# The lags of the filter: stored in the order of the products, or in the order of time

## The reference

```python
def hyena_filter_spectra(L, w_in, w_hid, b, freq, w_out):
    ...
    for k, w in enumerate((w_in, w_hid[0], w_hid[1])):
        hdn = jnp.sin(freq[k] * (hdn @ w.astype(f32) + b[k]))
    h = (hdn @ w_out.astype(f32)).reshape(L, HY_ORDER, 2, HY_WIDTH)
    ...
    h = h * jnp.exp(-t * deltas)[:, None, None, :]
    hf, hb = h[:, :, 0], h[:, :, 1]
    k_circ = jnp.concatenate([hf[:1] + hb[:1], hf[1:], jnp.zeros_like(hf[:1]), hb[:0:-1]], axis=0)
    return jnp.fft.rfft(k_circ, axis=0)
```

## Time and profile before

| | us |
|---|---|
| median of three runs | 4332.37 |
| the profiled execution | 4332.37 |
| its span | 4330.7 |
| outside the span | 1.67 |
| TensorE busy | 3802.4 (88%) |
| VectorE busy | 1439.4 (33%) |
| ScalarE busy | 899.4 (21%) |

### The profile page before, as it was taken

The page is one execution under the profiler, slowest core; times in us unless marked ns, Lnnn a source line. Parts: engine busy times, 40 slices in busy tenths (PEclk is TensorE's granted clock), DMA queues, the critical chain, the costliest instruction groups (busy, mean ns, idle before and its releaser), DMA issues. The chain is left out here.

```text
span 4330.7 us, 47795 instructions
## 1 busy us (share of the span) xinstructions
PE 3802.4 (88%) x18109; PEld 2658.2 (61%) x18109; DVE 1439.4 (33%) x2293; ACT 899.4 (21%) x1423; POOL 304.7 (7%) x278
## 2 busy tenths in 40 slices
PE   8798999994899999999978586998799959999995
PEld 2587888882666776677656354676466734444442
DVE  3124445445333443344333442232311241111112
ACT  1323333322122222122212242101111120000000
POOL 0400000000000000000000000221210000000001
PEclk9899999996999999999999687999899969999997
DMA  9100000101100000000011400001211128888885
GB/s 337 54 10 26 16 1 16 64 20 47 56 27 27 0 27 26 26 1 26 26 70 51 186 0 25 20 19 58 59 44 54 39 94 333 332 340 338 334 338 219
DMA packets 160410, 410.13 MB, mean 95 GB/s; under 512 B 14345, under 2 KB 97399, under 8 KB 147703
## 3 DMA queue, kind: packets, MB, share of 16 engines
q1 hardware_dynamic: 147244, 361.93, 22.9%
q0 software_dynamic: 8064, 29.36, 1.9%
q10 hardware_dynamic: 4972, 16.90, 1.0%
HBM read 347.35 MB, written 58.72 MB: 94 GB/s over the span
## 5 line engine op out<-in xcount | busy, mean ns | idle before, releaser
L1615 PE MATMUL hyena_up<-aT,ring 128*128 128x512 f32 x1024 | 465.6, 610 | 67.5 <-DMA ring<-in_hy_w_in 67.5
L1615 PEld LDWEIGHTS hyena_up<-aT,ring 128*128 128x128 f32 x1024 | 196.4, 197 | 298.0 <-issue 298.0
L1592 DVE COPY ring<-hyena_bank 128x512 f32<-128x512 f32 x192 | 131.9, 691 | 294.4 <-PE hyena_bank L1657 116.3
L2196 PE MATMUL hgrn_proj<-xT,ring 128*128 128x512 f32 x384 | 169.4, 600 | 9.8 <-DMA ring<-in_w_in 9.8
L3026 DVE TENSOR_TENSOR moe_h<-moe_gate,moe_up 128x512 f32<-128x512 f32 x32 | 22.0, 689 | 420.0 <-PE moe_up L2937 420.0
L1116 PE MATMUL mla_scores<-ring,mla_v 128*128 128x128 f32 x1280 | 153.8, 275 | 3.7 <-DVE ring L1019 3.7
L1116 PEld LDWEIGHTS mla_scores<-ring,mla_v 128*128 128x128 f32 x1280 | 148.0, 192 | 4.7 <-DVE ring L1019 4.7
L1519 ACT ACTIVATE ring<-hyena_bank 128x512 f32<-128x512 f32 x192 | 115.9, 603 | 164.1 <-PE hyena_bank L1657 60.4
L2196 PEld LDWEIGHTS hgrn_proj<-xT,ring 128*128 128x128 f32 x384 | 73.0, 193 | 97.7 <-issue 97.7
L1636 PE MATMUL hyena_bank<-ring,hyena_fwd 128*128 128x128 f32 x1088 | 126.6, 276 | 0.3
L1636 PEld LDWEIGHTS hyena_bank<-ring,hyena_fwd 128*128 128x128 f32 x1088 | 124.0, 192 | 2.3 <-DVE hyena_conv L1565 1.9
(11 more groups left out here) (548 smaller groups left out, 7452.5 us busy)
## 6 DMA issues: line engine op xcount, KB each, us to landing
ring<-in_w_gate_experts SPq DMA_DIRECT2D x16, 2048.0 KB
ring<-in_w_up_experts SPq DMA_DIRECT2D x16, 2048.0 KB, 17.1
ring<-in_w_down_experts SPq DMA_DIRECT2D x16, 2048.0 KB
aT<-in_w_gate_experts SPq DMA_DIRECT2D x16, 2048.0 KB, 12.9
aT<-in_w_up_experts SPq DMA_DIRECT2D x16, 2048.0 KB, 17.4
moe_w_spare<-in_w_down_experts SPq DMA_DIRECT2D x16, 2048.0 KB, 9.0
ring<-in_ada_w SPq DMA_DIRECT2D x12, 2048.0 KB, 9.4
ring<-in_hy_w_in SPq DMA_DIRECT2D x32, 512.0 KB, 6.6
```

The source lines that it names most:

```text
L1592: ins = dve.tensor_copy(*copy_out(name, k, ps))
L1615: mm = pe.matmul(up[j % 2][:, cols], w_in[:, k, j, :], m.aT[:, k, cols], start=(k == 0), stop=(k == KT - 1))
L2196: mm = pe.matmul(bank[:, :], w[:, KINDS.index(n), kt, :], m.aT[:, kt, half * BANK:(half + 1) * BANK], start=(kt == 0), stop=(kt == KT - 1))
```

## The change

`lags` is kept in time order. The sine then writes three plain rectangles in place of four scattered ones, and `K` takes as its stationary operand every sixteenth element of the row (step 64 bytes) in place of 128 neighbours. The same numbers go into the same products.

```diff
-                by_tile = m.lags[:, :].rearrange("p (g q) -> p q g", g=16)
-                in_time = arg[:, :].rearrange("p (q g) -> p q g", g=16)
-                first, second = slice(0, HID), slice(HID, 2 * HID)
-                for rows, q, g in ((first, slice(0, HID), slice(0, 16)), (second, slice(HID + 1, P), slice(0, 16)),
-                                   (second, slice(HID, HID + 1), slice(1, 16)), (second, slice(0, 1), slice(0, 1))):
-                    act.activation(by_tile[rows, q, g], in_time[rows, q, g], ACT.Sin).then_inc(s_sin, 1)
+                for rows, lo, hi in ((0, 0, SEQ), (HID, SEQ + 1, NFFT), (HID, 0, 1)):
+                    act.activation(m.lags[rows:rows + HID, lo:hi], arg[rows:rows + HID, lo:hi], ACT.Sin)\
+                       .then_inc(s_sin, 1)
...
                         if name == "K":
                             for i in range(4):
-                                mm = pe.matmul(ps[:, i * P:(i + 1) * P], m.lags[:, (4 * k + i) * P:(4 * k + i + 1) * P], w_lag[:, o, :],
+                                mm = pe.matmul(ps[:, i * P:(i + 1) * P], m.lags[:, 4 * k + i:NFFT:16], w_lag[:, o, :],
                                                start=True, stop=True)
```

## The result

The changed kernel takes 4384.33 us (median of four runs, 4381.94 to 4388.6) against 4330.11 of the kernel before: a ratio of 1.0125, 95% interval 1.011 to 1.0139, or 54 us more. The forecast was 4331.1 us with a range of 4324 to 4362. What came is the second rival, to which the prediction gave 14% and the price of 54.8 us.

A forecast was written before the change was run, and what follows sets the result against it. TensorE, busy for 88% of the span, was taken to bound the kernel, ScalarE and VectorE the sine's stage. From 4332.37 us, -1.8 for the sine and +0.5 for K gave 4331.1 us; range for 8 in 10: 4324 to 4362.

The forecast's parts named there:

- Rival 2: K's loads: the step halves their rate, distance 219 ns, +54.8 us, 4385 us, slower by 1.2%; chance 14%.
- The sine: End of the filter stage: three plain pieces take 2.14 us in place of 3.93, in full on the path, -1.8 us.
- K's place: K in the eight convolution passes: the load sets the distance, 111.9 ns, and nothing covers a longer one.
- K's price: K's 512 loads: the step adds 1 ns each, as Tv's 112.5 ns suggests, +0.5 us.
- The prediction's own sign of being wrong: Profile after: K's 32 loads take over 4.2 us, or the sine still takes 3.9 us.
- The bounds: Sine's gain 1.6 to 2.0 us; K's cost 0 to 4.1 us, the high end from 120 ns per load.
- the likeliest case: Whole kernel: sine gains, K's loads barely grow; 4331.1 us, own range 4326 to 4339 us; chance 67%.
- Rival 1: K's loads: the step adds a transpose's 53 ns each, +27.1 us, 4357.7 us, slower by 0.6%; chance 14%.
- Rival 3: Half-clock stretches or anything else shifting with the earlier start gives more than 8.7 us back; chance 3%.
- Rival 4: Behind the filter stage's barrier: DMAs land when they do, the sine's gain does not arrive, 4332.9 us; within the 67%.
- What moves beside it: Half-clock stretches after each pass's wait for weights: 0.6 us each, seven passes, up to 4.2 us either way.

The follow-up runs named there:

- the first series: The kernel before, with sixteen extra products or transposes of two moving columns, side by side or stepped, ahead of each job of K; one execution, 4755.72 us.

## Why the prediction was wrong, point by point

- **The sine: right.** -1.8 us was forecast; the pieces save 1.71 us (3.93 to 2.22), and the next stage starts that much sooner after the range reduction. That its end is the path was right too. In the whole time no run shows it: the two kernels with the gain alone came out at 1.0005, with 1.7 us less at the edge of the interval.
- **K's place: right.** The load sets K's distance, nothing covers it, and its price reaches the end: 54.4 us of loads, 54.2 us between the medians (1.0125, with an interval of 48 to 60 us, so the closeness of the two is luck), and about half of it for half of the loads.
- **K's price: the step that failed.** The prediction said: "If that slow rate is a floor for either reason, K stays at it", and took Tv's 112.5 ns as what K would have, so 512 x 1 ns = +0.5 us. It came to 512 x 106.2 ns. Two things were wrong with it. That the step cost Tv only 3.1 ns was cover: plain transposes stand 109 ns apart for their matmuls, and uncovered the step takes a transpose from 62 to 110 ns (medians). And Tv's time was not K's: with a step a transpose's load takes 110 to 120 ns and a product's 217 to 268, from 4 elements on. A product's slow rate side by side (107 ns of columns) is no floor under which the step's price hides; its distance doubles once each column lies in 16 bytes of its own, in one-pass products too. The prediction's own sign of being wrong, over 4.2 us for K's 32 loads, came out at 6.98.
- **The bounds.** The high end of the likeliest case (120 ns) came from another transpose, with a step of 16 bytes. Uncovered, a transpose's load takes 120 ns with that step too; so it was right for transposes and bounded nothing for a product (233 ns).
- **Rival 2: the number came, its reason did not.** A doubling of 192 - 85 ns was priced at 54.8 us and 7.0 us for K's 32 loads; 54.2 and 6.98 were measured. The reason given for it, a load that takes each element twice, is not borne out: one-pass products have the same 112 ns and double as well (233). And that it is so near is in part luck: by 16 elements the step adds 106 ns, by 4, 8 and 12 elements 121, 126 and 156 (8 and 12 read at 0.50). Both ends of the unknown cost belonged into the range and only one was in it.
- **Rival 1** (53 ns, 4357.7 us) is out: the load pays 106. **Rival 3** (a faster kernel) is out. **Rival 4** is out: the first matmul moved up with the sine.
- **What moves beside it: the size about right, the cause in part wrong.** Up to 4.2 us either way were put on the half-clock stretches at the heads of the passes. Kernels with the same loads differ by 4.6 us in this stage (1176.2 against 1180.9), and in the changed one 5.8 us stand beside K's price. But the part of the clock is about 1 to 3 us of it, the largest single piece lies in the middle of the first pass, and the waits for the weights, for which the prediction had no term, make up 1.8 to 3.8 us.

## What to carry to other kernels

A product's stationary operand wants its columns side by side, or at most 8 bytes apart in f32: in a product each load of 128 f32 columns took 119 ns with a step of 8 bytes and 175 with 12, and from 16 bytes on 217 to 268, instead of 112. Move the permutation to where it is done once, here into a table or a sine's output at 1.7 us, rather than into 512 loads. And when a neighbour's row is taken as the price of an operation, look first at what limits that neighbour: an operation that hides under another shows the other's time. The durations of the transposes' loads (141 and 194 ns) told more than their distances: 53 ns apart, where the step costs 48 uncovered. And a price holds for the kind of load it was read from: a product's load paid 106.

## What the hardware did that was not expected

- A product's load with a step of 4, 5 or 16 elements does not follow TensorE's clock: 233, 220 and 218 ns at 1.00, 233, 220 and 217 at 0.50. Side by side, and with 2 or 3 elements, it does: 112, 119 and 175 ns at 1.00, 213 at 0.50. So at the half clock this change would have cost about 4 ns per load and not 106, an estimate from the first series (217 - 213).
- A transpose's load loses most of its advantage already at a step of 2 elements (118 ns against 62), where a product's load hardly notices (119 against 112).
- One-pass loads in the rounded type take as long as those of a full product, 112 ns, and 233 with a step of 4.
- ScalarE writing with a step of 512 bytes took 1929 ns for 1024 elements against 1056 in a row.
